# Output projection: both token halves of six of the eight tiles behind one prepared weight tile

## The reference, cut to what matters

```python
mixed = jnp.concatenate([rmsnorm(o_sb, sb_out_norm_g[l]),
                         rmsnorm(o_mla, mla_out_norm_g[l])], axis=-1)
h = h + jnp.einsum('bse,ed->bsd', mixed, w_o[l])     # output projection
# then: u = rmsnorm(h, mlp_norm_g); h = h + relu(u @ w_up)^2 @ w_down; final norm
```

## Time and profile before

| | us |
|---|---|
| median of 3 runs | 3327.67 |
| the runs | 3328.99, 3319.13, 3327.67 |
| profiled execution, own time | 3327.38 |
| profiled execution, span | 3325.5 |
| mean granted clock of TensorE | 0.981 |

### The profile page before, as it was taken

How to read it: one execution, slowest core, us unless ns; L and a number is a source line. 1 busy time by engine, 2 the same in 40 slices (tenths; PEclk the granted TensorE clock), 3 DMA queues, 4 the chain that set the end, 5 groups by cost and what they waited for, 6 DMA issues and landing times. The chain is left out here.

```text
span 3325.5 us, 36569 instructions
## 1 busy us (share of the span) xinstructions
PE 3172.2 (95%) x14817; PEld 2458.5 (74%) x14817; DVE 1484.6 (45%) x1852; ACT 1152.5 (35%) x1690; POOL 742.8 (22%) x352
## 2 busy tenths in 40 slices
PE   6999999989999999998999999999999999999997
PEld 4765544677888888877667778888777678888885
DVE  4114345555222232475366766666645322333245
ACT  4234444333121121342463333333444442323233
POOL 2122211143222222243121010102111122222234
PEclk9999999999999999999999999999999999999998
DMA  3212000031111111234432111113333343132124
GB/s 122 103 45 83 32 1 16 2 120 60 50 51 45 51 51 45 65 116 147 107 121 83 39 61 57 67 51 104 118 111 105 108 159 113 58 114 97 61 92 136
DMA packets 113823, 263.50 MB, mean 79 GB/s; under 512 B 9209, under 2 KB 50425, under 8 KB 113529
## 3 DMA queue, kind: packets, MB, share of 16 engines
q1 hardware_dynamic: 104440, 228.93, 21.3%
q10 hardware_dynamic: 9216, 32.25, 2.4%
HBM read 199.80 MB, written 60.29 MB: 78 GB/s over the span
## 5 line engine op out<-in xcount | busy, mean ns | idle before, releaser
L1208 POOL TENSOR_TENSOR w_lo<-raw,w_hi 128x1024 fp32r<-128x1024 f32 x114 | 277.0, 2430 | 738.0 <-ACT w_hi L953 691.2
L1926 PE MATMUL psum<-normed_hi,w_hi 128*128 128x512 f32 x984 | 423.8, 431 | 14.7 <-PEq L184 9.0
L2428 POOL TENSOR_TENSOR w_lo<-raw,w_hi 128x1024 fp32r<-128x1024 f32 x64 | 173.1, 2705 | 974.8 <-ACT w_hi L1568 974.8
L1928 PE MATMUL psum<-normed_hi,w_lo 128*128 128x512 f32 x984 | 388.7, 395 | 0.0
L1927 PE MATMUL psum<-normed_lo,w_hi 128*128 128x512 f32 x984 | 387.6, 394 | 0.0
L3020 POOL TENSOR_TENSOR w_lo<-raw,w_hi 128x1024 fp32r<-128x1024 f32 x64 | 157.6, 2463 | 468.5 <-ACT w_hi L1568 466.8
L1568 ACT ACTIVATE w_hi<-raw 128x1024 fp32r<-128x1024 f32 x128 | 135.5, 1058 | 362.9 <-PE psum L2923 311.1
L1568 ACT ACTIVATE buffer<-psum,par 128x512 f32<-128x512 f32 (+1 forms) x191 | 133.9, 703 | 338.5 <-PE psum L1928 244.4
L2921 PE MATMUL psum<-normed_hi,w_hi 128*128 128x512 f32 x608 | 238.3, 392 | 12.6 <-PEq L184 9.7
L2922 PE MATMUL psum<-normed_lo,w_hi 128*128 128x512 f32 x608 | 237.2, 390 | 0.0
L2923 PE MATMUL psum<-normed_hi,w_lo 128*128 128x512 f32 x608 | 237.1, 390 | 0.0
(11 more groups left out here) (404 smaller groups left out, 6216.9 us busy)
## 6 DMA issues: line engine op xcount, KB each, us to landing
raw<-in_w_in SPq DMA_DIRECT2D x75, 512.0 KB, 4.5
raw<-in_w_mlp SPq DMA_DIRECT2D x72, 512.0 KB, 3.6
scratch_in<-buffer ACTq DMA_DIRECT2D x59, 512.0 KB, 2.7
buffer<-scratch_in SPq DMA_DIRECT2D x42, 512.0 KB, 4.6
raw<-in_w_gate SPq DMA_DIRECT2D x40, 512.0 KB, 3.7
buffer<-scratch_y SPq DMA_DIRECT2D x20, 512.0 KB, 8.1
raw<-in_w_br SPq DMA_DIRECT2D x20, 512.0 KB, 3.6
raw<-in_w_o SPq DMA_DIRECT2D x16, 512.0 KB, 3.6
```

The source lines that it names most:

```text
L1208: pool.tensor_tensor(ws.lo[:, n % 2], raw[:, n % 2], ws.hi[:, n % 2].bitcast(F32), ALU.subtract).then_inc(w_lo, 1)
L1926: pe.matmul(out, hi, xh, start=k == 0, stop=False)
L1928: mm = pe.matmul(out, lo, xh, start=False, stop=k == DC - 1)
L2428: pool.tensor_tensor(ws.lo[:, n % 2], raw[:, n % 2], ws.hi[:, n % 2].bitcast(F32), ALU.subtract).then_inc(w_lo, 1)
```

## The change: what it does

It replaces the order of the output projection. Tiles 0 and 1 are done for half 0 first (units 0, 1); then tiles 2 and 3 for half 0 and then for half 1 (units 2 to 5), likewise tiles 4, 5 (units 6 to 9) and 6, 7 (units 10 to 13); and tiles 0 and 1 for half 1 last (units 14, 15), with slots of their own. There are 10 slots for the 16 units instead of 16. The wait for `out_lo` 16 goes from unit 8 to unit 4. Residual transfers, squares and sums follow the new order, with their waits counted anew; `o_end[0]` becomes the end of unit 11 (it was that of unit 7), and `o_end[1]` stays the end of unit 15.

```diff
     def __init__(self):
         self.slots, self.units = [], []
-        self.passes("o", 0)
+        for tile in (0, 1):
+            self.slots.append(("o", tile))
+            self.units.append(FeedUnit("o", tile, 0, len(self.slots) - 1))
+        for first in range(2, DC, 2):
+            self.slots += [("o", first), ("o", first + 1)]
+            at = len(self.slots) - 2
+            self.units += [FeedUnit("o", first + t, h, at + t) for h in range(2) for t in range(2)]
+        for tile in (0, 1):
+            self.slots.append(("o", tile))
+            self.units.append(FeedUnit("o", tile, 1, len(self.slots) - 1))
...
-    o_end = [stream(DC * (h + 1)) for h in range(2)]
+    first_o = [next(j for _, j, half, _ in ff.units if half == h) for h in range(2)]
+    last_o = [[j for kind, j, half, _ in ff.units if (kind, half) == ("o", h)][-1] for h in range(2)]
+    o_end = [stream(ff.index("o", last_o[h], h) + 1) for h in range(2)]
...
+    def squares_added(n):
+
+        seen = [h for _, _, h, _ in ff.units[:n]]
+        return n - len(set(seen))
+
+    def square_used(n):
+
+        _, j, h, _ = ff.units[n]
+        return squares_added(n + 2 if j == first_o[h] else n + 1)
...
             def residual():
-                for h in range(2):
-                    cut = slice(h * HALF, (h + 1) * HALF)
-                    for j in range(DC):
-                        yield stream(h * DC + j) - 7.5
-                        n = h * DC + j
+                for n, (_, j, h, _) in enumerate(ff.units[:2 * DC]):
+                        cut = slice(h * HALF, (h + 1) * HALF)
+                        yield stream(n) - 7.5
...
-                            if n == DC:
+                            if n == 4:
                                 pe.wait_ge(out_lo, 16)
...
-                    pe.wait_ge(mlp_added, (DC - 1) * (h + 1))
+                    pe.wait_ge(mlp_added, squares_added(ff.index("o", last_o[h], h) + 1))
...
             def mlp_sums():   # ScalarE
-                for h in range(2):
-                    for j in range(DC):
-                        yield stream(h * DC + j + 1) + 1.0
-                        n = h * DC + j
+                for n, (_, j, h, _) in enumerate(ff.units[:2 * DC]):
+                        yield stream(n + 1) + 1.0
                         act.wait_ge(joined, added_by("o", j, h))
                         if n >= 2:
-                            act.wait_ge(mlp_added, sum_of(n - 2))
+                            act.wait_ge(mlp_added, square_used(n - 2))
...
             def mlp_sums():   # VectorE
-                for h in range(2):
-                    for j in range(1, DC):
-                        yield stream(h * DC + j + 1) + 1.8
-                        dve.wait_ge(mlp_squared, h * DC + j + 1)
-                        if j >= 2:
-                            dve.wait_ge(mlp_added, h * (DC - 1) + j - 1)
+                for n, (_, j, h, _) in enumerate(ff.units[:2 * DC]):
+                    if j != first_o[h]:
+                        yield stream(n + 1) + 1.8
+                        dve.wait_ge(mlp_squared, n + 1)
+                        if j != first_o[h] + 1:
+                            dve.wait_ge(mlp_added, squares_added(n))
```

More of the change, by code:

```diff
@@ L1462, in mlp_sums @@
             def mlp_sums():
-                for h in range(2):
-                    for j in range(1, DC):
-                        yield stream(h * DC + j + 1) + 1.8
-                        dve.wait_ge(mlp_squared, h * DC + j + 1)
-                        if j >= 2:
-                            dve.wait_ge(mlp_added, h * (DC - 1) + j - 1)
-                        dve.tensor_tensor(sums[h], squares[:, 0] if j == 1 else sums[h], squares[:, j % 2], ALU.add).then_inc(mlp_added, 1)
+                for n, (_, j, h, _) in enumerate(ff.units[:2 * DC]):
[4 more added lines that the diff above has]
+                            dve.wait_ge(mlp_added, squares_added(n))
+                        dve.tensor_tensor(sums[h], squares[:, 0] if j == first_o[h] + 1 else sums[h], squares[:, j % 2],
+                                          ALU.add).then_inc(mlp_added, 1)
             def mlp_scales():
```

## The result

| | before | after |
|---|---|---|
| median, us | 3327.2 (11 runs, 3319.13 to 3329.65) | 3333.66 (11 runs, 3328.83 to 3336.96) |
| profiled execution, own time, us | 3327.38 | 3332.29 |
| unit 0's first matmul to unit 16's first, us | 654.68 to 764.70: 110.0 | 654.90 to 770.23: 115.3 |

The ratio is 1.0021, 95% interval [1.0014, 1.0029]: slower by 4.7 to 9.6 us, less than the 0.3% I had named as the bound of "no change", and clear of zero. Forecast: 3330.6.

What follows compares the result with a forecast made beforehand. TensorE, busy 95% of the span, was taken to set the time. Early wait +5.0, slow stretch -0.7 and L892 -1.1 summed to +3.2 us on 3327.38, thus 3330.6 us, called "no change"; range 3319 to 3338.

Steps and rivals of the forecast that it cites:

- one more unit behind the gap: After TensorE's restart at unit 4, 12 units would be left where 11 were left from unit 5: +5.43 us.
- restart of TensorE: Unit 4 would start at 693.4 us, where unit 5 had started at 693.86: -0.46 us.
- slow stretch behind the first gap: Low-clock matmuls after the gap before unit 4 would cost 1.9 us, less than before: -0.7 us.
- L892 without a wait: Half 0's L892 matmul, now in unit 12, would no longer wait for VectorE's sum: gain 1.1 us.
- second gap moves unchanged: The w_lo gap before unit 11 would stand before unit 15 instead, at the same length: 0 us.
- The early wait: The out_lo 16 wait at unit 4 would idle TensorE 10 us until the norm's low parts end: +5.0 us.
- Residual transfers, sums in the new order: Transfers and sums of the reordered units would keep the same number and due times: 0 us.
- Cover of half 0's norm: Four units, not eight, would still cover half 0's MLP norm before unit 16, by 5 us at its start: 0 us.
- The second gap closes: Rival: with less GpSimd work the gap before unit 15 vanishes; 3324.4 us, chance 14%.
- the moved wait costs nothing: Rival: low parts are ready when unit 4 wants them, so the first gap goes; 3318.8 us, chance 12%.
- The norms run into each other: Rival: both halves' MLP norms share VectorE and GpSimd, delay showing in unit 18; 3337.6 us and above, chance 11%.
- The saved transfers count: Rival: six fewer weight transfers save time, which would need a DMA bound; given no chance.

Runs made afterwards that it cites:

- first trace: The changed kernel's first profiled execution, against the kernel before: own time 3332.29 us, stretch from unit 0's to unit 16's first matmul 115.3 us against 110.0.
- second execution: The changed kernel run once more, unaltered: median 3332.88 us, ratio 1.0014 to the kernel before, stretch 113.7 us.
- sum late: The changed kernel with unit 12's square added to its half's sum 5.4 due-time units later on VectorE: 3331.31 us in one run.
- two early preparations: The changed kernel with the weights of slots 9 and 10 prepared 3.5 and 6.5 due-time units earlier: 3331.73 us, ratio 1.0012 to the kernel before.
- four singles: The changed kernel with four leading tiles done for half 0 alone instead of two, the out_lo 16 wait at unit 6: 3323.39 us, ratio 0.9991 to before.

## Why the prediction was right, point by point

The mechanism was as forecast: the earlier wait puts one more unit behind a longer gap that `attended_lo` ends. The size came out low. The forecast was +3.2 us; the two traces have +5.3 and +3.6 us of stretch, the medians +6.5 and +4.8. In the first trace three terms missed by 0.46, 0.7 and 0.84 us, all to the same side. The range, 3319 to 3338, has room for that, and for a gain as well, so that the median fell into it confirms little by itself. What confirms the working is the timeline, step by step.

| step | forecast, us | measured in the first trace, us |
|---|---|---|
| one more unit behind the gap | +5.43 | +5.43 |
| restart of TensorE | -0.46 | 0.0 |
| slow stretch behind the first gap | -0.7 | 0.0 |
| L892 without a wait | -1.1 | -1.1 |
| second gap moves unchanged | 0 | +0.64, and +0.2 for one more slow matmul |
| sum | +3.2 | +5.2 (stretch +5.3) |

**The early wait.** The place, the releaser and the cause of the gap were as forecast. Unit 4 restarted 39.19 us after unit 0's start, where unit 5 had started after 39.18: no gain of 0.46. The low parts took 6.27 us, not 5.84. I had taken the uninterrupted set of the earlier trace rows, and the pieces of the earlier trace rows, 6.42 us, were nearer. TensorE then started 0.15 us behind the last of them, where I had put 0.06.

**The slow stretch.** The term was mis-sized for the first trace: 12 slow matmuls behind a gap of 10.45 us, as behind 4.92. The second execution had 7 behind the same gap, which is -1.0 us (5 x 0.2). The count is not a function of the gap's length in these runs (3.35 us: 13; 3.60: 12; 3.61: 7 and 0; 10.45 and 10.46: 12, 12, 7, 6 and 6; 14.57: 12), so two rows were no ground for a trend. The rule I cited beside it from the Trainium skill's page "TensorE: Matmul & The Clock Gate" (section "HAM oscillation — how this bites in real kernels"), that an idle spell is paid again behind it, holds for all these gaps but one; its flat price would have given +3.9, nearer to the first trace, and the measured prices reach from 0 to 2.6 us.

**L892.** Right in size (743.67 to 744.13 is 0.46 us, was 1.56) and in cause: the sum took 0.69 us with GpSimd at rest. The rule of the Trainium skill's page "SBUF — State Buffer" (section "Who interferes with whom") agrees with that 0.69 us.

**The second gap.** It moved to unit 15 as forecast, but "the same relative order" was false in one instruction. Unit 12 is not the first of its half, so its square is added where unit 8 had none to add. The step "Residual transfers, sums in the new order: the same number at the same due times, 0 us" failed there: the number is the same, the due times are not. The run with the sum late shows it, 4.24 back to 3.61 us.

**Cover of half 0's norm.** Right: its last low part ended 21.4 us after L911 and unit 16 began 26.6 us after it, and unit 16 did not wait for `normed_lo` in any variant either. The start without the second gap is misreckoned in the prediction: 25.7 - 6.2 is 19.5 us, not 19.1, and the cover 3.5 us, not 3. Nothing hangs on it.

**Rivals.** "The second gap closes" and "the moved wait costs nothing" did not occur. "The norms run into each other" did not occur in the changed kernel but is real: two early preparations called it up. "The saved transfers count" did not occur: the DMA share fell to 0.25 and the stage became longer.

What stays open: why single executions differ by 10 us outside the stage, what decides the number of slow matmuls behind a gap, and how much pairs bring once every late preparation in the order before is moved.

## What to carry to other kernels

Sharing a prepared operand between two halves saves work on the helpers, but it also asks for the second half's input earlier; price the earliest consumer's wait before the saved loads. A gap in TensorE that ends with a helper's instruction, while that helper is mostly idle over the stage, has two possible causes, and the helper's own timeline tells them apart. In the gaps of 4.92 and 3.60 us the preparation stood behind unrelated work, which is queue order: move it ahead. In the gap of 10.45 us GpSimd sat idle for 12.17 us and then did just what TensorE waited for. That is a chain of dependent steps. What helped here was an earlier start of the chain (the gap fell to 7.70 us) and other work for TensorE meanwhile (four singles). Then look at the next preparation and at the work pushed back, since here the gap moved on by one unit twice, and once it came back as a wait of another engine's sum.

## What the runs showed of the hardware that I had not expected

The same kernel, with the same gap (10.45 and 10.46 us), had 12 slow matmuls (0.427 us apart, not 0.227) behind it in one execution and 7 in another. Gaps of 3.60 or 3.61 us in three traces were followed by 12, 7 and none. A gap of 3.35 to 14.57 us thus cost 0 to 2.6 us (13 x 0.2) on top of its length in these traces, and one trace does not tell which.
